# A block of index keys widened by columns of v, three transposes turned one position on, attention units at spacing 6

## What is computed

```python
def _attn_mixer(xn, w_in, w_out, rel_bias):
    qa, ka, va, qd, kd, vd = jnp.split(xn @ w_in, ...)      # six blocks of 512 columns
    out_sb = _stick_breaking_attention(qa, ka, va)          # 8 heads of 64
    out_dil = _dilated_attention(qd, kd, vd, rel_bias)      # 8 heads of 64
    return jnp.concatenate([out_sb, out_dil], -1) @ w_out
# stick-breaking: log_keep = log_sigmoid(-z) where causal, a reverse cumulative sum of it over the keys,
# weights exp(log_sigmoid(z) + later), then weights @ v

def second_block(...):                                      # for each of two layers
    p = rms_norm(x) @ w_in      # b, c, xin, gate | q, k, v, gate, iq, ik, iw | pool u, gate | 3 merge gates
    y_a = short_conv_mixer(...)                             # b * conv(c * xin) * silu(gate)
    y_b = sparse_attention_mixer(...)
    y_c = pool_mixer(...)
    x = x + (g0 * y_a + g1 * y_b + g2 * y_c) @ w_o
# sparse attention: q and k are normed per head and rotated, iq (8 heads of 64) and ik (64) rotated;
# score = sum over heads of relu(iq . ik / 8) * iw, the top 64 keys of each query are kept,
# then a softmax attention over them, times silu(gate), @ w_out
```

## Time and profile before

| | |
|---|---|
| median of three runs | 1687.64 us |
| profiled execution | 1685.32 us, span 1683.5 us |
| TensorE matmuls (PE) | 1628.2 us busy, 97% |
| TensorE weight loads (PEld) | 1328.3 us, 79% |
| VectorE (DVE) | 970.6 us, 58% |
| ScalarE (ACT) | 810.2 us, 48% |
| mean granted TensorE clock | 0.989 |

### The profile page before, as it was taken

The page is one execution under the profiler, slowest core; times in us unless marked ns, Lnnn a source line. Parts: engine busy times, 40 slices in busy tenths (PEclk is TensorE's granted clock), DMA queues, the critical chain, the costliest instruction groups (busy, mean ns, idle before and its releaser), DMA issues.

```text
span 1683.5 us, 19537 instructions
## 1 busy us (share of the span) xinstructions
PE 1628.2 (97%) x7593; PEld 1328.3 (79%) x7593; DVE 970.6 (58%) x1218; ACT 810.2 (48%) x1014; POOL 50.7 (3%) x95
## 2 busy tenths in 40 slices
PE   7999999889999999999999999999999999989999
PEld 6888777678887788878777888787778878777887
DVE  4554566465455555466556554557945565794554
ACT  5543465254444543446655443455354535535552
POOL 2000000000000000000000000001000000100000
PEclk9999999999999999989999999999999999999999
DMA  9644644135547453544435544654424446442443
GB/s 300 219 145 178 222 175 150 50 127 185 174 145 255 164 198 137 189 163 151 149 113 190 176 158 169 202 208 150 150 100 150 150 174 239 150 150 101 148 152 125
DMA packets 187061, 279.29 MB, mean 166 GB/s; under 512 B 8525, under 2 KB 98805, under 8 KB 186992
## 3 DMA queue, kind: packets, MB, share of 16 engines
q1 hardware_dynamic: 184720, 271.27, 46.2%
q0 software_dynamic: 2128, 7.04, 1.4%
q10 hardware_dynamic: 144, 0.03, 0.0%
HBM read 277.26 MB, written 1.06 MB: 165 GB/s over the span
## 4 chain that ended last, share of the span: by engine, by line
PE 79%; DVE 13%; ACT 5%; issue 2%; POOL 1%; DMA 0%; POOLq 0%; SPq 0%; ACTq 0%; DVEq 0%
PE ACC L738 20%; PE ACC L740 20%; PE ACC L739 20%; DVE WL L1891 5%; PE TB L769 2%; PE ZB L914 2%; ACT WH L1304 2%; PE ACC L947 2%; PE ACC L949 1%; PE ACC L948 1%; PE ACC L1047 1%; PE ACC L1049 1%; PE ACC L1048 1%; ACT XH L1335 1%; PE ZB L917 1%
## 5 line engine op out<-in xcount | busy, mean ns | idle before, releaser
L1891 DVE TENSOR_TENSOR WL<-RAW,WH 128x2048 fp32r<-128x2048 f32 (+3 forms) x258 | 508.1, 2012 | 271.8 <-ACT WH L1304 267.5
L738 PE MATMUL ACC<-WL,XH 128*128 128x512 f32 (+2 forms) x1312 | 518.2, 395 | 16.8 <-issue 6.5
L740 PE MATMUL ACC<-WH,XL 128*128 128x512 f32 (+2 forms) x1312 | 509.4, 388 | 0.0
L739 PE MATMUL ACC<-WH,XH 128*128 128x512 f32 (+2 forms) x1312 | 508.7, 388 | 0.0
L1304 ACT ACTIVATE WH<-RAW 128x2048 fp32r<-128x2048 f32 (+3 forms) x258 | 422.4, 1687 | 163.4 <-PE ACC L740 109.3
L738 PEld LDWEIGHTS ACC<-WL,XH 128*128 128x128 f32 x1312 | 249.7, 190 | 75.0 <-issue 14.7
L740 PEld LDWEIGHTS ACC<-WH,XL 128*128 128x128 f32 x1312 | 249.5, 190 | 51.3
L739 PEld LDWEIGHTS ACC<-WH,XH 128*128 128x128 f32 x1312 | 249.9, 190 | 47.1
L738 PE MATMUL ACC<-WL,HH 128*128 128x512 f32 x352 | 138.1, 392 | 0.5
L740 PE MATMUL ACC<-WH,HL 128*128 128x512 f32 x352 | 137.1, 389 | 0.0
L739 PE MATMUL ACC<-WH,HH 128*128 128x512 f32 x352 | 137.1, 389 | 0.0
(11 more groups left out here) (293 smaller groups left out, 1800.2 us busy)
## 6 DMA issues: line engine op xcount, KB each, us to landing
RAW<-w_in_in SPq DMA_DIRECT2D x68, 1024.0 KB, 6.5
RAW<-ffn_w_gate_in SPq DMA_DIRECT2D x43, 1024.0 KB, 5.2
RAW<-ffn_w_up_in SPq DMA_DIRECT2D x43, 1024.0 KB, 7.4
RAW<-ffn_w_down_in SPq DMA_DIRECT2D x32, 512.0 KB, 4.5
RAW<-ffn_w_down_in SPq DMA_DIRECT2D x16, 1024.0 KB, 6.8
RAW<-mlstm_w_in_in SPq DMA_DIRECT2D x16, 1024.0 KB, 7.2
RAW<-ffn_w_down_in SPq DMA_DIRECT2D x16, 768.0 KB, 5.7
RAW<-attn_w_in_in SPq DMA_DIRECT2D x12, 1024.0 KB, 6.1
```

The lines of the kernel that those rows point to most:

```text
L738: nc.tensor.matmul(bank, lh, wl[:, i, :], start=first and i == 0, stop=False)
L739: nc.tensor.matmul(bank, lh, wh[:, i, :], start=False, stop=False)
L740: mm = nc.tensor.matmul(bank, ll, wh[:, i, :], start=False, stop=last and i == k - 1)
L1891: nc.vector.tensor_tensor(WL[:, slot, lo:hi], RAW[:, slot, lo:hi], WH[:, slot, lo:hi].bitcast(F32), ALU.subtract).then_inc(lo_ready, 1)
```

## The change

In `mix2` the block ik_iw gets, ahead of its own 72 columns, the second half of v's columns (256); the block v keeps the first half. Its chunk is loaded by two DMAs of these two column ranges, and its evacuation writes both the index keys and the V tile. The tasks q and k move from slots 10 and 14 to 11 and 15, conv_gate and split 0 from 20 to 21. In `attn` units 0 to 7 start at q = 37 + 6 u with shorter delays, units 8 and 9 are placed in block 5, the tail is written anew, each group of the output product waits for its own `mixed` group, which waits for four units, and the two scans of the logits become one.

```diff
-        SIZES = [(KD, IKW) if kind == "ik_iw" else (4, COLS) if kind == "branch" else FULL for kind in ORDER]
+        WIDTH = {"ik_iw": COLS // 2 + IKW, "v": COLS // 2}
+        SIZES = [(4 if kind == "branch" else KD, WIDTH.get(kind, COLS)) for kind in ORDER]
...
-        task(10, "q")
+        task(11, "q")
         task(12, ("rotate", "k"))
-        task(14, "k")
+        task(15, "k")
...
-        task(20, "conv_gate", ("split", 0))
+        task(21, "conv_gate", ("split", 0))
...
             for u in range(HEADS):
-                q = 2 * KD * 2 + KD + 7 * u
-                for delay, name in ((0, "scores"), (3, "logits"), (6, "weights"), (8, "turn"), (9, "masked"), (12, "weigh"),
-                                    (13, "taken")):
-                    if q + delay < 2 * KD * 6:
-                        place(q + delay, name, u)
+                q = 2 * KD * 2 + 5 + 6 * u
+                for delay, name in ((0, "scores"), (3, "logits"), (5, "weights"), (7, "turn"), (8, "masked"), (11, "weigh"),
+                                    (12, "taken")):
+                    place(q + delay, name, u)
+            for u in (8, 9):
+                q = 2 * KD * 5 + 6 + 5 * (u - 8)
+                for delay, name in ((0, "scores"), (2, "logits"), (3, "weights")):
+                    place(q + delay, name, u)
+            place(2 * KD * 5 + 12, "turn", 8)
+            place(2 * KD * 5 + 13, "masked", 8)
...
-            order += [("evacuate", 5, 1), ("turn", 7), ("masked", 7), ("scores", 8), ("logits", 8), ("hi", 7, 0), ("weights", 8),
-                      ("weigh", 7), ("taken", 7), ("turn", 8), ("scores", 9), ("masked", 8),
-                      ("mixed", 0), ("mixed", 1), ("logits", 9), ("weights", 9), ("lo", 7, 0), ("hi", 7, 1),
-                      ("weigh", 8), ("taken", 8), ("lo", 7, 1)]
+            order += [("evacuate", 5, 1), ("mixed", 0), ("mixed", 1), ("turn", 9), ("masked", 9), ("weigh", 8), ("scores", 10),
+                      ("logits", 10), ("weights", 10), ("taken", 8)]
             for n in range(2 * KD):
-                u = 10 + n // 2
-                if n % 2 == 0 and u < 2 * HEADS:
-                    order += [("turn", u - 1), ("scores", u), ("masked", u - 1), ("logits", u), ("weights", u), ("weigh", u - 1),
-                              ("taken", u - 1)]
-                if n == KD + 5:
-                    order += [("turn", 15), ("masked", 15)]
+                if n % 2 and n < 10:
+                    u = 11 + n // 2
+                    order += [("turn", u - 1), ("scores", u), ("masked", u - 1), ("logits", u), ("weights", u)]
+                    if n == 1:
+                        order += [("weigh", 9), ("taken", 9)]
+                elif 2 <= n <= 10:
+                    u = 9 + n // 2
+                    order += [("weigh", u), ("taken", u)]
+                order += {2: [("hi", 7, 0)], 3: [("lo", 7, 0)], 7: [("mixed", 2)], 8: [("hi", 7, 1)], 11: [("turn", 15), ("masked", 15)],
+                          12: [("lo", 7, 1)], 13: [("weigh", 15), ("taken", 15)], 15: [("mixed", 3)]}.get(n, [])
                 order.append(("part", 0, n // KD, n // 4 % 2, n % 4))
-            order += [("weigh", 15), ("taken", 15), ("mixed", 2), ("mixed", 3)]
...
+                    elif kind == "ik_iw":
+                        c, half = at.chunk, COLS // 2
+                        dst = tiles(c % 2, KD, half + IKW)
+                        src = w_in_2[layer].rearrange("(k p) n -> p k n", p=P)
+                        load(c, c % 2, c - 1, [(dst[:, :, 0:half], src[:, :, W2["v"] + half:W2["v"] + COLS]),
+                                               (dst[:, :, half:], src[:, :, W2["ik_iw"]:W2["ik_iw"] + IKW])])
+                        at.chunk += 1
...
-                    if half == 0 and tok == 0 and k % 4 == 0:
-                        pe.wait_ge(groups_used, g0 + ATTN_GROUP["mixed", 2 * second + 1, 0] + 2)
+                    if half == 0 and tok == 0 and k % 2 == 0:
+                        pe.wait_ge(groups_used, g0 + ATTN_GROUP["mixed", k // 2, 0] + 2)
...
-                          (o_used, u0 + HEADS * (g // 2 + 1)))
+                          (o_used, u0 + 4 * (g + 1)))
...
+                    elif kind in ("ik_iw", "v"):
+                        half = COLS // 2
+                        heads = slice(HEADS // 2, HEADS) if kind == "ik_iw" else slice(0, HEADS // 2)
+                        for tok in range(NTOK):
+                            block_ready(tok, at.chunk, at.block)
+                            src = ACC[:, (at.block % 2) * 2 + tok, :]
+                            if kind == "ik_iw":
+                                nc.scalar.activation(XN[:, tok, COLS:COLS + IKW], src[:, half:half + IKW], ACT.Copy,
+                                                     scale=RX[:, tok:tok + 1])
+                            ins = nc.scalar.activation(V2[:, tok, heads, 0:DH], src[:, 0:half].rearrange("p (h e) -> p h e", e=DH),
+                                                       ACT.Copy, scale=RX[:, tok:tok + 1])
+                        ins.then_inc(blocks_used, 1)
...
-                    for lo, hi in ((0, P), (P, 3 * P)):
-                        ins = nc.vector.tensor_tensor_scan(l[:, lo:hi][:, ::-1], goes_on[:, lo:hi][:, ::-1],
-                                                           a[:, lo:hi][:, ::-1], 0.0, ALU.mult, ALU.add)
-                    step(ins)
+                    step(nc.vector.tensor_tensor_scan(l[:, ::-1], goes_on[:, ::-1], a[:, ::-1], 0.0, ALU.mult, ALU.add))
```

More of the change, by code:

```diff
@@ L694, in mix2 @@
                         out_half += 1
+                    elif kind == "ik_iw":
[5 more added lines that the diff above has]
+                        at.chunk += 1
                     else:
-                        load_cols(w_in_2[layer], 0, KD, W2[kind], IKW if kind == "ik_iw" else COLS)
+                        load_cols(w_in_2[layer], 0, KD, W2[kind], WIDTH.get(kind, COLS))
             sp.dma_start(CT[:, 0:P], c_tiles[:, 0:P]).then_inc(ident_loaded, 16)
@@ L1275, in mix2 @@
                         break
-                    xh, xl, k, n = (BH, BL, 4, COLS) if kind == "branch" else (XH, XL, KD, IKW if kind == "ik_iw" else COLS)
+                    xh, xl, k, n = (BH, BL, 4, COLS) if kind == "branch" else (XH, XL, KD, WIDTH.get(kind, COLS))
                     if b == 0:
@@ L1702, in mix2, with take_out @@
                              pooled=lambda: plain(PL), attn_out=attn_out)
-                def take_out(dst, func, n=COLS):
+                def take_out(dst, func):
                     for tok in range(NTOK):
                         block_ready(tok, at.chunk, at.block)
[L1707 to L1712, removed]
+                        ins = nc.scalar.activation(dst[:, tok, :], ACC[:, (at.block % 2) * 2 + tok, :], func, scale=RX[:, tok:tok + 1])
                     ins.then_inc(blocks_used, 1)
```

## The result

| | before | after |
|---|---|---|
| median | 1687.71 us | 1669.61 us (4 runs, 1666.92 to 1672.61) |
| profiled execution | 1685.32, span 1683.5 | 1672.61, span 1670.8 |

The ratio is 0.9871 (95% interval 0.9844 to 0.9899): 18.1 us less by the medians, 12.7 less from profile to profile. A later series gave 1670.65 against 1689.71, ratio 0.9886 (0.9860 to 0.9912). The forecast was 1670.2, 17.4 less.

What follows compares the result with a forecast made beforehand. TensorE, busy 97% of the span, was taken to bound the kernel. Gains of 6.5 + 3.3 + 2.2 + 2.2 + 3.25 = 17.4 us gave 1667.9 for the profiled execution, 1670.2 by the median; range 1664 to 1677.5.

Steps and rivals of the forecast that it cites:

- The pair of blocks: In mix2, ik_iw and v with 328 and 256 columns take 13.0 us: 6.5 less in layer 0, 3.3 in layer 1.
- The moves: In mix2, q, k and gate transposes one position on: 2.2 us less per layer, of 5.7 and 5.4 in waits.
- pu's wait: In mix2, block pu would start at 1208.2 but waits for its first WL half until 1209.8.
- VectorE's chain: In mix2, VectorE's nearly unbroken work from k's rotation to cb's evacuation begins 1.1 us later and delays blocks cb and pu.
- Attention: In attn, 8.0 us lost in the tail go, 4.75 of new waits come: gain 3.25, bounds 7 and -1.
- turn 7: In attn, a new wait of 0.5 us behind staged 4.
- weigh 0: In attn, first product after block 2, at position 48, waits for that block's V to be evacuated: 0.95 us.
- scores 3: In attn, a new wait of 1.1 us behind lo(4,0), which stands ahead of logits 2 in VectorE's order.
- scores 1: In attn, a new wait of 0.6 us behind lo(3,1).
- turn 9: In attn's new tail, a wait of 0.6 us for the first mixed group's lo.
- turn 10: In attn's new tail, a wait of 1.0 us for the exp after scores 10, with one part product as cover.
- Rival 3: Clock falls all the same, behind attn's block 5 or where pu waits 1.7 us: 3.4 us, 1673.6; chance 0.14.

Runs made afterwards that it cites:

- the late rotation: The changed kernel with VectorE's rotation of q put behind the sums of index 0 and 1 in slot 8: 1663.62 us against 1689.59, ratio 0.9840.

## Why the prediction was right, and where not

**The pair of blocks: right.** 6.5 and 3.3 forecast, 6.54 and 3.33 measured; so was the pace of 0.150 and 0.120. Keeping the excess over the columns' own time whole was the right way between the bounds. What I did not see is that layer 1's undisturbed pair was luck: I had one profile, with a fall in one layer and none in the other, and took both for what the kernel does.

**The moves: right, term by term.** 2.2 per layer, measured 2.2 in both. q lost 0.88 (forecast 0.9), pu's wait moved its block by 1.66 (1.6), cb's by 0.1 (0.2). The reading that held is "what is late next": of 5.7 and 5.4 us of waits at their face value, 3.5 and 3.2 stood in front of something else that was nearly as late. That the slower clock behind k's wait (booked at 1.9, by the blocks 1.6) is part of those 5.7 but worth nothing is borne out too, since the gate's wait was shorter by as much.

**VectorE's chain: right where it mattered, too rigid as a picture.** It binds between cc and the gate. But my text spoke of it as a thing that only its own work moves. The chain hangs on the block that TensorE ends before it, so a gain ahead of it passes through whole, as the late rotation showed.

**Attention: the sum near, its terms not.** Forecast 3.25, measured 4.15 in the two profiles, 3.3 of it idle time. The forecast was 8.0 of losses that go, 1.5 of them the clock, less 4.75 of new waits; the new waits were 3.15, and of the clock only 0.9 came back (busy time 140.5 to 139.6). Of the waits booked, turn 7 (0.5) did not appear; weigh 0 was 0.8 (0.95), scores 3 0.8 (1.1), scores 1 0.2 (0.6), turn 9 1.2 (0.6), turn 10 0.2 of idle time (1.0 booked, under the lower clock). The step that failed is the count of work between mixed 0 and turn 9: Rival 3 has 19 transposes in a row there, but they are 8, then the wait for `XL`, then turn 9's 3. Eight transposes, 0.11 us apart, are 0.9 us of cover that wasn't there. So the sign that I gave, waits for `UW` near 1 us and none for `XL`, came out the other way round: 0.2 for `UW`, 1.2 for `XL`. The misses partly cancel, which is luck.

**What the sum lacked: the clock.** Added up by block, the change gave 6.5 + 3.3 + 2.2 + 2.2 + 4.15 = 18.4 in the profiled executions, not 17.4, and 5.9 went elsewhere, which leaves 12.5 of the 12.7: three falls of 1.5 to 1.6 (mlstm, block iq of layer 1, `index 4` of layer 1) and 1.2 of small differences in stages that are as before. The last of the falls stands behind the wait of `index 4`, 1.46 us long now that no transposes lie under it. My text implies that wait (the slot ends when it did) but does not name it as a place for a fall. It is one: of 14 such waits in seven profiles 6 were followed by a fall (five cost 1.5 to 1.6, one 3.2), and of the 12 passages without that bare wait none. Rival 3 named pu's wait instead; behind its 1.4 us no fall came in any of 14. In the tail of attn, which it also named, the clock did fall, but it had done so before the change as well, and longer.

So the hit of the median, 1669.6 to 1670.2, is closer than the reasoning deserves: the kernel before has medians of 1687.6 to 1692.1 in different series. The ratio, 0.987 to 0.989, is the firmer figure; 17.4 us is 0.9897.

**Left open.** Why one execution loses its clock in a place where the next one does not, with the same waits in front; only its share of cases was counted. The 1.4 us of idle time before pu and the 1.5 before `index 4` look alike and behave differently. One thing that differs is what follows: behind `index 4`'s wait come the eight 64-row matmuls of two heads, 1.7 us long, behind pu's at once the full ones of a block. No run separates that from the place.

## What to carry to other kernels

Read a wait together with what would be late next, and then move the work that makes the next thing late: k and the gate on their own were worth 6.4 us, and reordering VectorE's work behind them another 8. Where only one part of a move has a wait to remove, move that part: q gained nothing and cost 2 us. With a clock that falls now and then behind short waits, one profile gives the waits but not their price; compare block by block, count falls over several executions, and value a wait removed at its length plus the price of a fall times the share of passages in which one follows.

## What the runs showed of the hardware

- A matmul of fp32r with a fresh load of 128 weight columns costs 0.110 us at 72 columns and 0.111 at 200, and its columns at 2.4 GHz plus 13 to 14 ns from 256 on (0.120, 0.150, 0.174, 0.228 at 256, 328, 384, 512).
- 72-column matmuls back to back, TensorE busy throughout, were followed by the lower clock in 5 of 6 cases; 200-column ones at the same pace in none of 2, those of 328 and 256 in none of 18.
- Two heads' scores on 64 rows each run side by side (starts 0.01 us apart, both done in 0.95); behind separate waits they take 1.8.
- A fall of the clock ahead of a wait that VectorE sets cost nothing: 26.75 + 11.81 + 14.25 = 52.8 with it, 25.15 + 11.77 + 15.85 = 52.8 without.
